# Unrolled layers, attention in pairs of heads, sigmoids on ScalarE and low weight parts on VectorE in a two-layer hybrid decoder

## Chip, cores and metric

One core of a Trainium2 chip runs the kernel. The metric is the device time of one launch in microseconds (us). Engines are called as in the profile: PE is TensorE, DVE is VectorE, ACT is ScalarE, POOL is GpSimd, SP is SyncE, which here only issues DMAs.

## What is computed

Two layers of a decoder trunk on 512 tokens of width 1024, in float32. A combined input projection feeds three kinds of token mixing (latent attention, called A; an mLSTM matrix memory, B; dilated sliding-window attention, C), then come cross-attention to 256 memory tokens and a SwiGLU of inner width 2816. Each sub-layer has an RMS norm before and one after it, ahead of the residual add.

```python
def reference(x, mem, w_in, ...):
    ...
    for l in range(DEPTH):
        h = rms_norm(x, norm_mix_pre[l])
        (c_q, c_kv, k_rope, ml_q, ml_k, ml_v, ml_o, ml_i, ml_f,
         sw_q, sw_k, sw_v) = jnp.split(h @ w_in[l], splits, axis=-1)
        y_a = mla_mixer(c_q, c_kv, k_rope, ...)          # 8 heads, dense causal, values of 64
        y_b = mlstm_mixer(ml_q, ml_k, ml_v, ml_o, ...)   # silu(conv(q, k)); sigmoid(ml_o) * h
        y_c = dilated_swa_mixer(sw_q, sw_k, sw_v, ...)   # 4 heads of 64
        y = jnp.concatenate([y_a, y_b, y_c], axis=-1) @ w_out[l]
        x = x + rms_norm(y, norm_mix_post[l])
        h = rms_norm(x, norm_x_pre[l])
        y = memory_cross_attention(h, rms_norm(mem, norm_mem[l]), x_w_q[l], x_w_kv[l], x_w_o[l])
        x = x + rms_norm(y, norm_x_post[l])
        h = rms_norm(x, norm_ffn_pre[l])
        y = swiglu(h, w_gate_up[l], w_down[l])
        x = x + rms_norm(y, norm_ffn_post[l])
    return x
```

## The kernel before

**Layout.** Activations are feature-major: `x` is 8 tiles (`KT`) of 128 features by 512 tokens, and all of them stay in SBUF. All 128 weight units of a layer (`N_UNITS`), each 128x1024 floats, stream through a ring of four slots (`RING`): units 0 to 21 are input, query, key and value weights of the mixing, from `U_OUT` = 22 the output projection, 30 and 38 the memory's keys and values, 46 the cross query, 54 the cross output, from `U_FF` = 62 gate and up, from `U_DOWN` = 106 the down projection.

**Three matmuls for one.** Every projection keeps nearly float32 accuracy with rounded operands: an operand is split into a high part and the rest, and PE adds three products (`three`, L552 hi by hi, L553 lo by hi, L554 hi by lo). So each unit takes three steps before PE can use it: SP loads it to `raw`, ACT makes `w_hi` (L853), and another engine subtracts to get `w_lo`. That is DVE (L1102) for units 2 to 21 and POOL (L522) for all from `U_OUT` on, and POOL (L451 and the layer's end) for units 0 and 1. A slot is loaded again once its low part is made; it is split again once PE has used the unit. Activations are split in the same way: ACT writes `h_hi`, DVE `h_lo` (L1152 for inputs whose norm factor is applied after the projection; L1128 and L1133, `tn_x` and `h_lo`, where it is applied ahead).

**Norms.** ACT squares a tile into one of two `sq` buffers (L865), DVE adds it to `acc` (L1112, L1114), PE sums over the partitions with a matrix of ones (L597), and ACT makes `rstd` with a logarithm and an exponential (L876). After an output projection, `residual` scales each `y` tile by `rstd` (L1163) and adds it to `x` (L1168); in the second and third residual, POOL adds tiles 1, 3, 4 and 6 (`POOL_ADDS`, L528).

**Order.** Each engine has its program written out by hand in blocks: a first block loads the memory and prepares the first units, then a hardware loop (`nc.Fori`) runs one block per layer and after it one that clears all semaphores of the layer, with a jump back; a last block stores `x` in one DMA (L1521). In a layer: `h_hi`/`h_lo` of all x tiles; the input projection, two output tiles together at first (L622 turns the first norm's factors right after the third tile); convolution and silu of the mLSTM's queries and keys; mLSTM loop of 16 steps (4 heads by 4 key blocks; spreads over four rows, scores L677, numerators L685, weights L1341) with the query, key and value projections between its steps; mixing attention of 12 heads (8 A, 4 C); output projection with the memory's norm; residual; keys and values of the memory, which PE can do without `x`; `x_pre` norm (first all eight squares, then eight norm steps); cross-query projection; cross-attention; its output projection; residual with the input of the FFN; FFN; down projection; residual.

**Sigmoids.** `silu` of the convolutions and the output gate are 1/(1+exp(-v)): ACT makes the exponential, DVE adds one and takes the reciprocal (`silu`, L1212 and L1326 for `o_gate`). In the FFN it is the same (L1477).

**Mixing attention** takes one head at a time, four query blocks each: PE scores (L747), DVE masks and takes the row's extreme (L1404), ACT exponentiates, DVE divides, PE transposes the probabilities (L725, three units behind), ACT copies them out, and two units later the head's value product (L753) runs over four key blocks, with an output of 64 partitions. DVE makes the head's `h_lo` (L1423).

## Time and profile before

| | |
|---|---|
| median of 3 runs | 1825.67 us (1823.3 to 1828.65) |
| profiled execution, its own time | 1825.33 us |
| its span in the trace | 1823.5 us |
| mean granted clock of PE | 0.954 |
| busy PE / DVE / ACT / POOL | 92% / 57% / 37% / 31% |
| moved by DMA | 146.5 MB, mean 80 GB/s |

One execution was recorded by the hardware profiler. Times in its rows are in us from the start of the span, if not marked ns. A group of instructions is named by its line in the kernel, its engine, and output<-inputs. In brackets behind a row stands how long the engine had waited before it and for which instruction. "Granted clock" is the share of full speed at which PE was let run: 1.00 is 2.4 GHz, 0.50 is 1.2 GHz. The rows themselves follow behind the change.

### The profile page before, as it was taken

Reading aid. Unit: us, or ns where it says so; the run is one execution under the profiler, and the core shown is the slowest. Engines: PE = TensorE matmul, PEld = TensorE weight load, DVE = VectorE, ACT = ScalarE, POOL = GpSimd, SP = SyncE. Lnnn points to the kernel's source line nnn. Section 1 sums busy time; section 2 is a strip of 40 time slices with the busy share of each in tenths; the row PEclk is TensorE's granted clock in tenths of the full one; section 3 lists DMA queues with packets and bytes.
Section 4 is the critical chain, followed back from the end, with each engine's and each line's share of the span. In section 5 each row is a group of like instructions: output and inputs, shape, how many; then the busy total and the mean of one; then the engine's idle time right before and its main releaser. Section 6 shows DMA issues by size and latency. Waiting matters only on the chain.

```text
span 1823.5 us, 20537 instructions
## 1 busy us (share of the span) xinstructions
PE 1669.0 (92%) x7040; PEld 1267.5 (70%) x7040; DVE 1046.6 (57%) x1511; ACT 675.2 (37%) x1148; POOL 565.9 (31%) x240
## 2 busy tenths in 40 slices
PE   6998899889989999999689988998899899999994
PEld 5864457767667888888468554477677678888883
DVE  5968872752257776600378678727531678765003
ACT  5322674444443332222143216644343432332221
POOL 1000103562234454444300001036613434444442
PEclk9989999999999999999889889998999999999997
DMA  5210002341112332223023110033412123222221
GB/s 224 93 60 33 24 1 104 105 137 59 58 46 91 105 102 95 102 93 103 25 95 104 36 35 13 1 116 105 137 47 69 55 84 109 98 96 100 102 95 58
DMA packets 39099, 146.50 MB, mean 80 GB/s; under 512 B 4976, under 2 KB 4976, under 8 KB 38256
## 3 DMA queue, kind: packets, MB, share of 16 engines
q1 hardware_dynamic: 39024, 145.53, 23.3%
q8 instruction: 44, 0.72, 0.2%
q14 instruction: 31, 0.25, 0.0%
HBM read 143.41 MB, written 2.10 MB: 80 GB/s over the span
## 4 chain that ended last, share of the span: by engine, by line
PE 41%; DVE 5%; issue 2%; POOL 1%; ACT 1%; DVEq 0%; POOLq 0%; ACTq 0%
PE bank L552 11%; PE bank L554 11%; PE bank L553 11%; PE bank L753 2%; PE bank L747 1%; POOL w_lo L522 1%; PE bank L725 1%; DVE tn_x L1128 1%; PE bank L794 1%; PE bank L784 1%; PE bank L677 1%; PE bank L685 1%; DVE y_f L1163 0%; DVE o_gate L1326 0%; PE bank L597 0%
## 5 line engine op out<-in xcount | busy, mean ns | idle before, releaser
L522 POOL TENSOR_TENSOR w_lo<-raw,w_hi 128x1024 fp32r<-128x1024 f32 x212 | 518.8, 2455 | 1175.9 <-ACT w_hi L853 1175.9
L552 PE MATMUL bank<-h_hi,w_hi 128*128 128x512 f32 x1312 | 534.4, 407 | 68.0 <-DVE h_lo L1152 39.9
L553 PE MATMUL bank<-h_lo,w_hi 128*128 128x512 f32 x1312 | 520.2, 396 | 0.0
L554 PE MATMUL bank<-h_hi,w_lo 128*128 128x512 f32 x1312 | 519.3, 396 | 0.0
L853 ACT ACTIVATE w_hi<-raw 128x1024 fp32r<-128x1024 f32 x256 | 268.1, 1050 | 223.9 <-PE bank L554 223.7
L552 PEld LDWEIGHTS bank<-h_hi,w_hi 128*128 128x128 f32 x1312 | 252.3, 192 | 140.5 <-issue 55.6
L553 PEld LDWEIGHTS bank<-h_lo,w_hi 128*128 128x128 f32 x1312 | 252.8, 193 | 55.6 <-issue 3.9
L554 PEld LDWEIGHTS bank<-h_hi,w_lo 128*128 128x128 f32 x1312 | 252.1, 192 | 53.8
L1114 DVE TENSOR_TENSOR acc<-acc,sq 128x512 f32<-128x512 f32 x86 | 73.3, 852 | 322.4 <-ACT sq L865 320.7
L1477 DVE RECIPROCAL acc<-acc 128x512 f32<-128x512 f32 x44 | 147.5, 3353 | 1.5
L552 PE MATMUL bank<-a_hi,w_hi 128*128 128x512 f32 x352 | 138.7, 394 | 0.0
L554 PE MATMUL bank<-a_hi,w_lo 128*128 128x512 f32 x352 | 138.0, 392 | 0.0
L553 PE MATMUL bank<-a_lo,w_hi 128*128 128x512 f32 x352 | 136.6, 388 | 0.0
L1079 ACT ACTIVATE a_hi<-sq 128x512 f32 (+1 forms) x44 | 27.8, 632 | 252.0 <-DVE sq L1481 252.0
L865 ACT ACTIVATE sq<-bank 128x512 f32<-128x512 f32 x48 | 28.7, 598 | 146.9 <-PE bank L554 146.9
L554 PEld LDWEIGHTS bank<-a_hi,w_lo 128*128 128x128 f32 x352 | 66.1, 188 | 15.5
L553 PEld LDWEIGHTS bank<-a_lo,w_hi 128*128 128x128 f32 x352 | 66.1, 188 | 14.8
L552 PEld LDWEIGHTS bank<-a_hi,w_hi 128*128 128x128 f32 x352 | 66.2, 188 | 13.1
L1404 DVE CUSTOM_DVE_ANT_0 p_x<-bank,consts 128x256 f32<-128x256 f32 x32 | 13.6, 425 | 90.3 <-PE bank L784 89.4
L1011 ACT ACTIVATE p_mix<-p_mix,stat 128x128 f32<-128x128 f32 (+1 forms) x96 | 53.6, 558 | 27.0 <-DVE stat L1404 26.7
L961 ACT ACTIVATE w_ml<-w_ml 128x512 f32<-128x512 f32 (+3 forms) x32 | 15.0, 470 | 130.4 <-DVE w_ml L1352 130.4
L1404 DVE CUSTOM_DVE_ANT_0 p_mix<-bank,consts 128x128 f32<-128x128 f32 (+1 forms) x96 | 47.2, 492 | 21.4 <-PE bank L747 15.5
(185 smaller groups left out, 2205.1 us busy)
## 6 DMA issues: line engine op xcount, KB each, us to landing
raw<-w_in SPq DMA_DIRECT2D x248, 512.0 KB, 3.3
raw<-first_in SPq DMA_DIRECT2D x12, 512.0 KB, 3.5
mem<-mem_in SPq DMA_DIRECT2D x3, 1024.0 KB, 4.9
x<-x_in SPq DMA_DIRECT2D x1, 2048.0 KB, 10.6
out<-x SPq DMA_DIRECT2D x1, 2048.0 KB, 6.3
consts<-c_in SPq DMA_DIRECT2D x1, 1728.0 KB, 14.3
gains<-g_in SPq DMA_DIRECT2D x2, 36.0 KB, 3.7
first_g<-first_g_in SPq DMA_DIRECT2D x3, 4.0 KB, 3.1
```

What stands on the lines that cost most here:

```text
L522: pool.tensor_tensor(w_lo[:, s, :], raw[:, s, :], w_hi[:, s, :].bitcast(F32), ALU.subtract).then_inc(split_lo, 1)
L552: pe.matmul(out_ap, l_hi, r_hi, start=start, stop=False)
L553: pe.matmul(out_ap, l_hi, r_lo, start=False, stop=False)
L554: return pe.matmul(out_ap, l_lo, r_hi, start=False, stop=stop)
L753: mm = pe.matmul(outs[head % 2][0:64, kb * P:SEQ], mix_head(head)["v"](kb), pt_mix[:, head % 2, kb, kb * P:SEQ], start=(kb == 0), stop=(kb ...
L853: act.activation(w_hi[:, s, :], raw[:, s, :], ACT.Copy)\
L865: act.activation(sq[:, c % 2, 0:width], src, ACT.Square).then_inc(squared, 1)
L1011: act.activation(probs[:, u % PROBS, 0:n], probs[:, u % PROBS, 0:n], ACT.Exp, scale=-1.0, bias=stat[:, 0, u:u + 1], accum_out=stat[:, 1, u ...
L1079: act.activation(a_hi[:, bass.ds(j * (2 * SEQ) + i * SEQ, SEQ)], f_a[:, i, :], ACT.Copy)\
L1114: ins = dve.tensor_tensor(acc[:, :], acc[:, :], sq[:, s, :], ALU.add)
L1404: done(dve.tensor_tensor_reduce(probs[:, u % PROBS, 0:n], score_ring[u % 4][:, 0:n], const(mask(u // TB) + SEQ - n, n), -scale(u // TB), 3 ...
L1477: step(dve.reciprocal(e, e), 2)
```

## The change

- **No loop over layers.** Both layers are written out in one block. Each semaphore counts on through the second layer (`count`, with the steps of a layer in `PER_LAYER`); no clearing, no first and last block. Inner loops of the FFN stay.
- **Start.** SP issues the first four weight units and the four quarters of `x` in turn; all gains come in one load. The memory for its norm factor is loaded behind unit 7 and its squares and column sums are made inside layer 0's input projection. Three output tiles are projected together (`HEAD`), with six banks in turn (`IN_BANKS`).
- **Layer handover.** The residual at the FFN's end also makes the next layer's `h_hi`, `h_lo` and squares (`next_input`). The result is stored in four quarters as its tiles are finished.
- **Latent norms.** The squares of the latent query and key tiles are summed over partitions by PE straight from `sq` (`latent_sum`), three matmuls for two, without an addition on DVE.
- **Sigmoids** outside the FFN: ACT makes exp, ln(1 + .), exp(-.) one after the other, and DVE only multiplies.
- **Low weight parts.** DVE makes units 4 to 65 (up to `U_FF` + 3), set beside its other work (`lo_until`, `beside`); POOL makes 0 to 3 and from 66 on. POOL adds nothing to `x` any more.
- **Mixing attention in pairs.** The steps of two heads go together (`pair_scores`, `pair_transposes`, `pair_out`); six probability buffers (`tn_mix` lends two). The value products of the two heads alternate and write partitions 0 to 63 and 64 to 127 of one bank, so one `h_hi`, one `h_lo` step serves a pair.
- **`x_pre` squares** are added inside the residual after the output projection (`x_square`).

```diff
-AHEAD = 2
-POOL_ADDS = (1, 3, 4, 6)
+HEAD = 3
+IN_BANKS = 6
 LAG = 3
 PROBS = LAG + 1
 OUT_LAG = 2
+PAIR_LAG = 2
+PAIR_PROBS = 2 * (PAIR_LAG + 1)
...
+    "mem_loaded": 16, "split_hi": N_UNITS, "split_lo": N_UNITS, "unit_used": N_UNITS,
+    "tile_done": tiles_done(len(USES) - 1),
...
+        def count(s, layer, n):
+            return layer * PER_LAYER[s.name] + n
...
+                for s in range(RING):
+                    sp.dma_start(raw[:, s, :], w_in[s, :, :]).then_inc(raw_loaded[s], 16)
+                    if s == 0:
+                        sp.dma_start(gains[:, :, :], g_in).then_inc(gains_loaded, 16)
+                    sp.dma_start(x[:, 2 * s:2 * s + 2, :], x_in[:, 2 * s:2 * s + 2, :]).then_inc(x_loaded[s], 16)
...
+                    for n in range(0 if layer else RING, N_UNITS):
+                        if layer == 0 and n == 2 * RING:
+                            sp.dma_start(mem_sq[:, :, :], mem_in).then_inc(mem_first, 16)
+                        if n == U_OUT + RING + 1:
+                            sp.wait_ge(mix_at["out_lo"], count(mix_at["out_lo"], layer, MIX_PAIRS))
+                            sp.dma_start(mem[:, :, :], mem_in).then_inc(mem_loaded, 16)
+                        load(first + n)
+                for i in range(KT // 2):
+                    sp.wait_ge(x_updated, count(x_updated, DEPTH - 1, N_SCALED - KT + 2 * i + 2))
+                    sp.dma_start(out[:, 2 * i:2 * i + 2, :], x[:, 2 * i:2 * i + 2, :]).then_inc(stored[i], 16)
...
+                def make_lo(u):
+                    pool.wait_ge(split_hi, u + 1)
+                    pool.tensor_tensor(w_lo[:, u % RING, :], raw[:, u % RING, :], w_hi[:, u % RING, :].bitcast(F32),
+                                       ALU.subtract).then_inc(split_lo, 1)
+                for layer in range(DEPTH):
...
+                    for n in list(range(RING)) + list(range(U_FF + RING, N_UNITS)):
+                        if n == U_FF + RING:
+                            pool.wait_ge(k_pe_ready, count(k_pe_ready, layer, 1))
+                            pool.wait_ge(ml_num, count(ml_num, layer, ML_HEADS * TB))
+                            pool.tensor_copy(k_mla[K_PE_ROWS[0], 2:MLA_HEADS, :], k_pe[K_PE_ROWS[0], :].unsqueeze(1)
+                                             .broadcast_to([MLA_ROPE, MLA_HEADS - 2, SEQ])).then_inc(k_pe_copied, 1)
+                            pool.wait_ge(k_pe_copied, count(k_pe_copied, layer, 1))
+                            wait_split(pool, layer, U_FF + RING - 1)
+                        make_lo(layer * N_UNITS + n)
...
-                    pool.wait_ge(k_pe_copied, 1)
-                    each_unit(pool, U_OUT + 2, U_FF + RING, make_lo)
-                    add_tiles("x_post", y_x)
-                    each_unit(pool, U_FF + RING, N_UNITS, make_lo)
...
+                    def latent_sum(name, first, n):
+                        pe.wait_ge(latent_squared, count(latent_squared, layer, first + n))
+                        pe.wait_ge(ln_done, count(ln_done, layer, NORM_AT[name]))
+                        for k in range(n):
+                            mm = pe.matmul(norm_bank[:, :], const(C_ONES), sq[:, k, :], start=(k == 0),
+                                           stop=(k == n - 1))
+                        mm.then_inc(norm_summed, 1)
...
                         after_norm("mix_pre")(k)
-                        for m in range(2):
+                        for m in range(HEAD):
                             project_step("in", m, k, tiles(h_hi), tiles(h_lo))
-                            if k == KT - 1 and m == 0:
-                                pe.wait_ge(consts_loaded, 16)
-                                norm_sum("mix_pre")
...
                         for kb in range(TB):
-                            mm = pe.matmul(outs[head % 2][0:64, kb * P:SEQ], mix_head(head)["v"](kb),
-                                           pt_mix[:, head % 2, kb, kb * P:SEQ], start=(kb == 0), stop=(kb == TB - 1))
+                            for i in range(2):
+                                mm = pe.matmul(outs[pair % 2][64 * i:64 * i + 64, kb * P:SEQ],
+                                               mix_head(2 * pair + i)["v"](kb), pt_mix[:, i, kb, kb * P:SEQ],
+                                               start=(kb == 0), stop=(kb == TB - 1))
                         mm.then_inc(mix_at["out"], 1)
-                    attention(mix_at, MIX_HEADS, p_mix, causal_len, mix_scores, mix_out)
...
-                    pe.wait_ge(mix_at["out_lo"], MIX_HEADS)
...
+                        if s < PAIR_STEPS:
+                            pair_scores(s)
+                        t = s - PAIR_LAG
+                        if t >= 1 and t % TB == 0:
+                            pair_out(t // TB - 1)
+                        if 0 <= t < PAIR_STEPS:
+                            pair_transposes(t)
...
-                        act.activation(o_gate[:, j, :], o_gate[:, j, :], ACT.Exp, scale=-1.0).then_inc(o_exp, 1)
+                        wait_emptied(act, layer, use_of("in", OG + j))
+                        e = o_gate[:, j, :]
+                        done(act.activation(e, e, ACT.Exp, scale=-1.0), act_step)
+                        done(act.activation(e, e, ACT.Ln, bias=one[:, :]), act_step)
+                        act.activation(e, e, ACT.Exp, scale=-1.0).then_inc(o_exp, 1)
...
+                def scaled_lo(layer, name, k, g):
+                    dve.wait_ge(normed_hi, count(normed_hi, layer, normed_before(name) + k + 1))
+                    done(dve.scalar_tensor_tensor(out=h_lo[:, k, :], in0=x[:, k, :],
+                                                  scalar=gains[:, layer, g + k:g + k + 1],
+                                                  in1=h_hi[:, k, :].bitcast(F32), op0=ALU.mult,
+                                                  op1=ALU.subtract), normed_lo)
...
-                        dve.wait_ge(conv_exp, j + 1)
-                        e = conv_in[:, j % 2, 3:3 + SEQ]
-                        done(dve.tensor_scalar(e, e, 1.0, None, ALU.add), dve_step)
-                        done(dve.reciprocal(e, e), dve_step)
-                        done(dve.tensor_tensor(ml_qk[:, j, :], ml_qk[:, j, :], e, ALU.mult), ml_qk_ready)
+                        dve.wait_ge(conv_exp, count(conv_exp, layer, j + 1))
+                        done(dve.tensor_tensor(ml_qk[:, j, :], ml_qk[:, j, :], conv_in[:, j % 2, 3:3 + SEQ], ALU.mult),
+                             ml_qk_ready)
...
-                    lo_until(U_OUT)
                     ml_denominator(ML_HEADS - 1)
                     ml_finish(ML_HEADS - 1)
                     for b in range(TB):
                         take_value(b)
                     ml_output_lo(1)
+                    lo_until(U_OUT + 3)
...
+                    dve.wait_ge(mem_loaded, count(mem_loaded, layer, 16))
                     mem_norm = (KT, tiles(mem), G_MEM, tiles(m_hi), tiles(m_lo))
-                    add_squares("mix_post", KT, between=lambda m: norm_step("mem", m, *mem_norm))
+                    add_squares("mix_post", KT, between=lambda m: norm_step("mem", m, *mem_norm),
+                                beside=lambda m: lo_until(U_OUT + m + 4))
...
+                    def x_square(k):
+                        lo_until(U_XK + k + 4)
+                        if k >= 1:
+                            add_square(layer, "x_pre", k - 1)
+                    residual("mix_post", "out", y_x, x_square)
+                    add_square(layer, "x_pre", KT - 1)
...
+                    dve.wait_ge(rstd_ready, count(rstd_ready, layer, NORM_AT["x_pre"] + 1))
+                    for k in range(KT + 1):
+                        norm_step("x_pre", k, KT, tiles(x), G_X_PRE, tiles(h_hi), tiles(h_lo))
+                        lo_until(U_XV + 7 + (k + 1) // 2)
...
+                    def next_input(k):
+                        if k >= 1 and layer + 1 < DEPTH:
+                            scaled_lo(layer + 1, "mix_pre", k - 1, G_MIX_PRE)
+                            add_square(layer + 1, "mix_pre", k - 1)
+                    residual("ffn_post", "down", y_f, next_input)
...
+                            dve.wait_ge(ff_lo, count(ff_lo, layer, j * 2 + (i + 1)))
+                    dve.wait_ge(rstd_ready, count(rstd_ready, layer, NORM_AT["ffn_pre"] + 1))
```

DVE, from the residual behind the output projection of the first layer to the first norm steps (y_x is the projection's output, acc and sq the sum and a tile of squares). Before:

```order
L1163 TENSOR_TENSOR y_x<-y_x,rstd 128x512
L1168 TENSOR_TENSOR x<-x,y_x 128x512
L1163 TENSOR_TENSOR y_x<-y_x,rstd 128x512
L1168 TENSOR_TENSOR x<-x,y_x 128x512 x2
L1112 COPY acc<-sq 128x512
L1114 TENSOR_TENSOR acc<-acc,sq 128x512 x7
L1128 SCALAR_TENSOR_TENSOR tn_x<-x,gains,rstd 128x512 x2
L1133 TENSOR_TENSOR h_lo<-tn_x,h_hi 128x512
L1128 SCALAR_TENSOR_TENSOR tn_x<-x,gains,rstd 128x512
L1133 TENSOR_TENSOR h_lo<-tn_x,h_hi 128x512
```

After, same place:

```order
L1250 TENSOR_TENSOR y_x<-y_x,rstd 128x512
L1254 TENSOR_TENSOR x<-x,y_x 128x512
L1231 TENSOR_TENSOR w_lo<-raw,w_hi 128x1024
L1173 COPY acc<-sq 128x512
L1250 TENSOR_TENSOR y_x<-y_x,rstd 128x512
L1254 TENSOR_TENSOR x<-x,y_x 128x512
L1231 TENSOR_TENSOR w_lo<-raw,w_hi 128x1024
L1175 TENSOR_TENSOR acc<-acc,sq 128x512
L1250 TENSOR_TENSOR y_x<-y_x,rstd 128x512
L1254 TENSOR_TENSOR x<-x,y_x 128x512
L1231 TENSOR_TENSOR w_lo<-raw,w_hi 128x1024
```

Each tile's scaling and add are now followed by a low weight part and the add of the last tile's square, where before no weight part stood on DVE and the eight squares came at the end.

PE, inside the mixing attention of group A in the first layer: scores from k_mla and q_mla, transposes of p_mix, value product from pt_mix and v_mla. Before:

```order
L747 MATMUL bank<-k_mla,q_mla 128x512
L725 MATMUL bank<-consts,p_mix 128x128
L747 MATMUL bank<-k_mla,q_mla 128x128
L725 MATMUL bank<-consts,p_mix 128x128 x2
L753 MATMUL bank<-pt_mix,v_mla 64x512
L753 MATMUL bank<-pt_mix,v_mla 64x384
L753 MATMUL bank<-pt_mix,v_mla 64x256
L753 MATMUL bank<-pt_mix,v_mla 64x128
L747 MATMUL bank<-k_mla,q_mla 128x256
L725 MATMUL bank<-consts,p_mix 128x128 x3
```

After:

```order
L732 MATMUL bank<-k_mla,q_mla 128x256 x2
L745 MATMUL bank<-consts,p_mix 128x128 x8
L732 MATMUL bank<-k_mla,q_mla 128x384 x2
L756 MATMUL bank<-pt_mix,v_mla 64x512 x2
L756 MATMUL bank<-pt_mix,v_mla 64x384 x2
L756 MATMUL bank<-pt_mix,v_mla 64x256 x2
L756 MATMUL bank<-pt_mix,v_mla 64x128 x2
L745 MATMUL bank<-consts,p_mix 128x128 x2
L732 MATMUL bank<-k_mla,q_mla 128x512 x2
```

Where a head's value product was four instructions with 64 output partitions between single scores and transposes, now eight stand together, two of each width, and scores and transposes come in twos as well.

DVE at the layers' border: the last tiles of the residual behind the down projection (y_f is its output). Before, where the block then ends:

```order
L1163 TENSOR_TENSOR y_f<-y_f,rstd 128x512
L1168 TENSOR_TENSOR x<-x,y_f 128x512
L489 UNCONDITIONAL_BRANCH
L1507 UNCONDITIONAL_BRANCH
L1510 ISA x20
L1496 UNCONDITIONAL_BRANCH
L488 REGISTER_ALU
L488 COMPARE_AND_BRANCH
```

After, the same residual of the first layer, near its start:

```order
L1250 TENSOR_TENSOR y_f<-y_f,rstd 128x512 x2
L1254 TENSOR_TENSOR x<-x,y_f 128x512
L1250 TENSOR_TENSOR y_f<-y_f,rstd 128x512
L1254 TENSOR_TENSOR x<-x,y_f 128x512
L1181 SCALAR_TENSOR_TENSOR h_lo<-x,gains,h_hi 128x512
L1173 COPY acc<-sq 128x512
L1250 TENSOR_TENSOR y_f<-y_f,rstd 128x512
L1254 TENSOR_TENSOR x<-x,y_f 128x512
L1181 SCALAR_TENSOR_TENSOR h_lo<-x,gains,h_hi 128x512
L1175 TENSOR_TENSOR acc<-acc,sq 128x512
L1250 TENSOR_TENSOR y_f<-y_f,rstd 128x512
```

The end of the block, 20 clearing instructions and the loop's branch stood between the last add and the next layer's first h_lo; now that h_lo and its square's add stand between the residual's own steps.

## Rows read from the trace of the kernel before

**Rows 1.** The page: busy time of each engine, share of the span, instructions.

```profile
PE 1669.0 (92%) x7040; PEld 1267.5 (70%) x7040; DVE 1046.6 (57%) x1511; ACT 675.2 (37%) x1148; POOL 565.9 (31%) x240
```

**Rows 2.** PE's waits: for whom: us, times, longest; then a window of the FFN.

```profile
PE bank L552 <- DVE h_lo L1152: 39.9, 4, 23.0
PE bank L552 <- POOL w_lo L522: 16.5, 5, 7.3
...
core 0: us, PE busy (x) PEld busy (x) DVE busy (x) ACT busy (x) POOL busy (x), PEclk, DMA share, GB/s
600.00:640.00 40.00, 40.00 (x178) 33.15 (x177) 31.55 (x29) 12.18 (x16) 18.98 (x9) 1.00 0.32 105
```

**Rows 3.** Start, order of time: start us, us, engine, line, what [idle before <-releaser].

```profile
7.79 6.02 PE L483 MATMUL bank<-mem_sq,ones_first 128*128 128x256 f32 x16 [7.79 <-ACT mem_sq L466]
8.66 4.65 POOL L451 TENSOR_TENSOR w_lo<-raw,w_hi 128x1024 fp32r<-128x1024 f32 x2 [8.21 <-ACT w_hi L469]
...
26.24 1.22 DVE L1102 TENSOR_TENSOR w_lo<-raw,w_hi 128x1024 fp32r<-128x1024 f32 x1
...
27.38 0.74 DVE L1152 SCALAR_TENSOR_TENSOR h_lo<-x,first_g,h_hi 128x512 fp32r<-128x512 f32 x1
...
39.77 1.05 PE L622 MATMUL bank<-consts,mix_rstd 1*128 1x1 f32 x8
```

**Rows 4.** Handover to the second layer, order of time, PE and DVE.

```profile
892.44 0.40 PE L554 MATMUL bank<-a_hi,w_lo 128*128 128x512 f32 x1
...
896.92 1.29 DVE L1163 TENSOR_TENSOR y_f<-y_f,rstd 128x512 f32<-128x512 f32 x2 [2.65 <-ACT rstd L876]
...
918.43 0.79 PE L552 MATMUL bank<-h_hi,w_hi 128*128 128x512 f32 x1 [22.98 <-DVE h_lo L1152]
...
940.35 1.05 PE L622 MATMUL bank<-consts,mix_rstd 1*128 1x1 f32 x8
```

**Rows 5.** Output to query projection, layer 0, order of time: POOL, then DVE.

```profile
333.30 16.71 POOL L522 TENSOR_TENSOR w_lo<-raw,w_hi 128x1024 fp32r<-128x1024 f32 x6 [6.49 <-ACT w_hi L853]
...
333.57 2.90 DVE L1168 TENSOR_TENSOR x<-x,y_x 128x512 f32<-128x512 f32 x1
...
374.47 4.59 DVE L1128 SCALAR_TENSOR_TENSOR tn_x<-x,gains,rstd 128x512 f32<-128x512 f32 x2 [8.44 <-ACT rstd L876]
...
394.16 1.42 DVE L1133 TENSOR_TENSOR h_lo<-tn_x,h_hi 128x512 fp32r<-128x512 f32 x2
```

**Rows 6.** mLSTM stage, order of time, then a window as in Rows 2.

```profile
120.71 3.35 DVE L1326 RECIPROCAL o_gate<-o_gate 128x512 f32<-128x512 f32 x1
...
152.36 0.79 PE L685 MATMUL bank<-w_ml,ml_v 128*128 128x128 f32 x2 [2.17 <-DVE w_ml L1341]
...
1087.56 2.49 DVE L1313 TENSOR_TENSOR o_gate<-o_gate,sq 64x512 f32<-64x512 f32 x1
...
1033.00:1037.00 4.00, 4.00 (x9) 2.11 (x9) 2.29 (x3) 1.58 (x2) 0.00 (x0) 0.50 0.01 2
```

**Rows 7.** Windows: four A heads, two C heads; DVE by shape; a product.

```profile
224.33:247.33 23.00, 23.00 (x104) 13.27 (x103) 19.55 (x69) 17.44 (x53) 0.00 (x0) 1.00 0.00 1
254.60:268.44 13.84, 13.84 (x53) 6.51 (x53) 9.74 (x35) 9.10 (x26) 0.00 (x0) 1.00 0.00 1
...
L1423 DVE TENSOR_TENSOR h_lo<-bank,h_hi 64x512 fp32r<-64x512 f32 x4 | 2.7, 683 | 0.1
...
L1404 DVE CUSTOM_DVE_ANT_0 p_mix<-bank,consts 128x256 f32<-128x256 f32 x4 | 1.7, 425 | 1.7 <-PE bank L747 1.7
...
247.67 2.37 PE L753 MATMUL bank<-pt_mix,v_mla 128*64 128x512 f32 x8
```

**Rows 8.** End, order of time; the page: DMA, count, KB, us to landing.

```profile
1812.54 0.69 DVE L1168 TENSOR_TENSOR x<-x,y_f 128x512 f32<-128x512 f32 x1
1816.44 0.35 SPq L1521 DMA_DIRECT2D out<-x  x1
...
raw<-w_in SPq DMA_DIRECT2D x248, 512.0 KB, 3.3
```

817 lines of the change are left out of this document (407 added, 410 removed).

## Prediction

> **What bounds the kernel now.** I read the page's first part, then who waits for whom on TensorE, then the order of time at the places where TensorE stands still. TensorE (PE) is busy 1669.0 of 1823.5 us [rows 1]; it sets the time, and the rest is gaps. The longest are on `h_lo` at the start and the layer handover (39.9 us in 4) and on low weight parts made by POOL (16.5 us in 5) [rows 2]. A second loss isn't idle time: in places PE runs at 1.2 GHz, granted clock 0.50 [rows 6], and does the same work in twice the time. In FFN and down projection it is dense at full clock, 178 matmuls touch a window of 40 us, 0.227 each [rows 2], and the change leaves them alone. The sum goes stage by stage, against the profiled execution's 1825.33 us, 0.34 below the median.
>
> **The change, part by part** (us; minus is gain; both layers together unless said).
>
> *Start: -6.9 +3.4.* Before, the third input tile is done at 39.7, where L622 follows [rows 3]. After, the memory's load and squares are out of the way, and three tiles are projected together. What is last is `w_hi[2]`: four activations on two x tiles stand ahead of each split on ACT (2.65), a split takes 1.0, so it is made by 4.2+1.0+2×(2.65+1.0)=12.5 (4.2: the first tile's landing, 3.3 after its issue [rows 8]), and POOL's low part takes 2.3 [rows 3]: 14.9. Then 66 matmuls, nine at half clock (3.9) and 57 at 0.228 (13.0), and the norm sum, 1.0: 32.8. The memory's column sums move from a time when PE had nothing to do into the dense stretch: 6.02 at half clock there [rows 3], 3.4 at full (8 matmuls, 256 columns, four passes). The latent norms' sums on PE add three fp32 matmuls for two, so 1 × 0.95 a layer: **+1.9**.
>
> *Handover: -17.9.* Last down matmul 892.44, `y_f` scaling from 896.92, first matmul of the next layer 918.43, its third tile done 940.4 [rows 4]. Block end, semaphore clearing and the jump back go; the next layer's `h_hi`/`h_lo` are made as each x tile is updated. DVE then does four steps a tile: scaling 0.65, add 0.69, `h_lo` 0.74 [rows 3, 4, 8] and the add of a square, as long as the other add; that is 2.77, and 2.82 from tile to tile with gaps; PE needs nine matmuls, 2.04: DVE paces. `h_lo[0]` at 901.0, `h_lo[7]` at 918.5, PE +2.0, norm sum +1.0: 921.5, against 940.4. POOL's last low part touches the first scalings: 1.0 back.
>
> *mLSTM stage: -15.* Six reciprocals a layer leave DVE, 3.35 each [rows 6]. The four of the convolutions buy nothing: PE is dense there and DVE only keeps up. The two output gates stand between mLSTM steps. Behind the second, PE stalls 2.17 in layer 0 [rows 6] and 2.24 at the same place of layer 1, and in stretches around such places it stays at half clock (0.50 in the window shown). In layer 0 the first gate is hidden by PE itself at half clock. From below: these stalls, 4.4. From above: the half-clock stretches also go, some 23 us in layer 0 and 34 in layer 1, half of each lost, 28 more. I take 12, near the low end, since the spread matmuls on four rows stay and half clock begins beside them too. With POOL quiet, DVE's slowed output product (2.49 for 0.69 [rows 6], and one like it in layer 0) gives 3. After the loop DVE makes three low parts (3×1.19) before the first mask, and loses 4.5 of slowing: nothing either way. ACT's new exp, ln, exp triples, two more steps of 0.65 each time, lie beside dense PE work on an engine that is 37% busy [rows 1]; without that cover they cost 1.3 each, 15.6.
>
> *Mixing attention: -18.* A head costs PE 5.75 (four in 23.0) in group A and 6.92 in C (two in 13.84), PE busy throughout [rows 7]. DVE is busy 19.55 in those 23.0 and waits 1.7 for scores, so unhindered it needs (23.0-1.7)/4=5.33 a head, less half an `h_lo` step (2.7/8=0.34): 4.99, 9.98 a pair. ACT is below that: 17.44/4=4.36. The value product, 2.37 for eight instructions on 128*64, i.e. half the array's columns [rows 7], becomes two interleaved ones on the two halves. No row shows whether they overlap: a pair costs 2.37 or 4.74. I take 2.37, since they share no column, output partition or operand. Then PE needs 11.5-2.37=9.1 a pair, DVE paces, and six pairs take 59.9 for 73.7 now: 13.8 a layer at best. I take 9: DVE, where it paces the mLSTM stage, is not gap-free, and a pair's drain adds a transpose group. If they don't overlap, group A gains nothing, C gains its halved switching between 64-row scores and full transposes (6.92-5.75=1.17 a head), the drain adds 2: about -2.5 a layer.
>
> The Trainium skill, "TensorEngine Tiling (Array Packing)", Key Properties, says that different tiles execute weight loads and matmuls in parallel; no run here shows it yet. By that the value product is the 2.37 I took.
>
> *Output projection to query projection: -26.* This is where POOL's low parts hurt twice. They come six in 16.71, 2.8 each, and DVE's adds beside them take 2.90 for 0.69 [rows 5, 8]. From 333.57 to 395.58 everything passes through DVE. After, DVE makes the parts itself, 1.22 each [rows 3]. Residual with squares: 0.61+0.70+1.19+0.72=3.2 a tile, 3.7 with the waits on ACT's squares (split 1.0, copy 0.4, square 0.6 are in line behind PE's 2.7 a unit); all squares added by 361, the fourth value unit's part 362, PE through it 364.8, sum 0.9, rstd 1.3: 367.0 where it was 374.47. Then eight steps of 1.51 and four parts of 1.19, `h_lo[7]` at 383.8: **11.8** less. Layer 1 took 4.8 longer for the same rows before, so 14.2 there.
>
> *FFN entry: -1.* DVE does all adds (2.82 a tile) but is no longer slowed. *End: -7.8.* Before: last add starts 1812.54, DMA issued 1816.44 after a block end [rows 8], span ends 1823.5. After: the last quarter is issued 0.4 after the last add's end (1812) and lands in 3.3 [rows 8]: 1815.7.
>
> **Sum:** -3.5+1.9-17.9-15-18-26-1-7.8=-87.3. **1738.**
>
> **Rivals.**
> 1. *Value products don't overlap.* For: PE's 64-row and full matmuls queue one by one in [rows 7]. Attention -5 for -18: **1751**. The Trainium skill, "TensorE: Matmul & The Clock Gate", The mechanism, says weight loads overlap running matmuls only when the row group differs; these halves share all rows. No row here shows it; by that the time would be this rival's.
> 2. *Full clock in the mLSTM stage.* With the gates gone PE has no gap over 1 us; -29 for -15: **1724**. Against: half clock also comes where PE was busy all the time, as in the window of [rows 6].
> 3. *DVE becomes the queue.* Low parts stand behind waits for squares: half of stage 5's gain and 7 of the mLSTM stage's are lost: **1758**.
> 4. *Slower.* A part waits for a split, that for PE's use of a unit, that for the part four ahead, with ACT's squares between. If ring slots didn't decouple them, each of 32 output and cross-output units (two layers) would take 1.22+1.05+5.44=7.7 for 5.44 and each of 32 key and value units 7.7 for 3.7: +72+128, **1938**; it passes 1825 from about 44% of that. Against: splits ran three units ahead in every stage.
> 5. *Nothing moves*, because the order compiled is the old one: 1825. The program's order speaks against it.
>
> **Chances.** Forecast 0.45 (its own range 1726 to 1746), rival 1 0.25, 2 0.12, 3 0.13, 4 0.03, 5 0.02. The range takes in 1 and 2 and, beyond 3, the lower ends of handover and attention (+10): **1716 to 1768**, leaving some 0.15 out. A measurement tells 0.3% apart; faster 0.95, same 0.02, slower 0.03.
>
> **What would show it.** Handover gap on PE near 8 us instead of 26. Value product of a pair near 2.4 and attention near 65 us a layer. No DVE step of 2.9 before the FFN. x_pre's first norm step 40 after the last output matmul, the last 57 after. Half-clock windows in the mLSTM stage fewer. Last `x` add to span's end 4 us. I am wrong if ACT's triples delay splits so that PE waits in the input projection, or if half clock spreads into attention once PE has slack there.

## The result and the profile after

The changed kernel takes **1755.38 us** (median of 4 runs, 1752.38 to 1756.94); the kernel before, run beside it, 1827.16 us. The ratio is 0.9608 with a 95% interval of 0.9591 to 0.9625. The profiled execution took 1754.44 us with a span of 1752.3, 71.2 less than the span before.

The page of the changed kernel, first the busy times, then two groups of its part on costly groups (busy us, mean ns):

```profile
PE 1631.1 (93%) x7044; PEld 1244.1 (71%) x7044; DVE 1027.5 (59%) x1568; ACT 677.8 (39%) x1156; POOL 325.5 (19%) x138
...
L489 POOL TENSOR_TENSOR w_lo<-raw,w_hi 128x1024 fp32r<-128x1024 f32 x132 | 319.8, 2427 | 1059.5 <-ACT w_hi L859 1059.5
...
L1231 DVE TENSOR_TENSOR w_lo<-raw,w_hi 128x1024 fp32r<-128x1024 f32 x124 | 150.9, 1225 | 101.9 <-ACT w_hi L859 90.0
```

PE is busy 37.9 us less than in [rows 1] and the gaps are 33.3 us less. POOL has 240 us less to do, and DVE makes 124 low parts at 1.22 us each.

Who waits for whom on PE (us in total, times, longest):

```profile
PE bank L510 <- DVE h_lo L1181: 21.1, 5, 8.9
PE bank L745 <- DVE p_mix L1510: 13.7, 14, 1.7
PE bank L510 <- DVE w_lo L1231: 7.5, 6, 1.3
PE bank L745 <- DVE tn_mix L1510: 6.1, 8, 0.9
```

The wait for `h_lo` is 21.1 us for 39.9 in [rows 2], and its longest is 8.9 for 23.0. The waits of transposes for probabilities of DVE, 13.7 and 6.1 us, are new: before, `p_mix` cost 3.8 us in all.

**Where the time went.** The order of time on PE and DVE has a row at each border. Those of the changed kernel, first layer and handover:

```profile
34.56 1.02 PE L557 MATMUL bank<-acc,consts 128*128 128x512 f32 x2
...
195.51 1.71 PE L732 MATMUL bank<-k_mla,q_mla 128*128 128x128 f32 x8
...
266.67 4.53 PE L756 MATMUL bank<-pt_mix,sw_v 128*64 128x512 f32 x16 [0.69 <-ACT pt_mix L1065]
...
359.52 1.54 DVE L1210 SCALAR_TENSOR_TENSOR tn_x<-x,gains,rstd 128x512 f32<-128x512 f32 x2 [2.42 <-ACT rstd L896]
...
425.12 3.60 PE L805 MATMUL bank<-pt_x,v_x 128*128 128x512 f32 x8
...
498.35 1.29 DVE L1250 TENSOR_TENSOR y_x<-y_x,rstd 128x512 f32<-128x512 f32 x2 [0.47 <-ACT rstd L896]
...
878.23 1.64 DVE L1250 TENSOR_TENSOR y_f<-y_f,rstd 128x512 f32<-128x512 f32 x2 [2.65 <-ACT rstd L896]
...
882.69 0.77 PE L510 MATMUL bank<-h_hi,w_hi 128*128 128x512 f32 x1 [5.94 <-issue]
...
903.05 1.02 PE L557 MATMUL bank<-acc,consts 128*128 128x512 f32 x2
```

The third input tile is done a norm sum after 34.56, at 35.6. That answers to the row at 39.77 in [rows 3], for L622 stands behind the third tile before and behind the fourth after.

| stage (from, to) | before, layer 0 / 1 | after, layer 0 / 1 | forecast, both | measured, both |
|---|---|---|---|---|
| start to third input tile | 39.8 | 35.6 | -6.9 | -4.2 |
| third tile to first attention score | 163.6 / 169.3 | 159.9 / 154.7 | -9.7 | -18.2 |
| attention, first score to last value product | 77.7 / 77.7 | 75.7 / 73.0 | -18 | -6.7 |
| to the first cross-attention value product | 164.9 / 163.5 | 153.9 / 153.9 | -26 | -20.6 |
| to the scaling of `y_f` | 450.8 / 450.7 | 453.1 / 452.9 | -1 | +4.4 |
| handover, `y_f` to third tile | 43.4 | 25.8 | -17.9 | -17.6 |
| last `y_f` scaling to the span's end | 22.0 | 13.7 | -7.8 | -8.3 |
| sum | | | -87.3 | -71.2 |

(The second row's forecast is mLSTM -15, latent norms +1.9 and the memory's column sums +3.4, which the prediction counted at the start.) Single stages in one profile differ by up to 3.5 us from kernel to kernel where nothing was changed in them: the second row's stage takes 154.7 us in layer 1 of the changed kernel and 154.8 to 158.2 in the eight kernels of experiments 1, 2, 7, 8, 9 and 10, which run the same program there. Its profile is the lowest of these, so some 2 us of that row's gain may be chance. The experiments are read with that in mind.

### The profile page after: what moved, and what is told of

It reads as the page before. It is cut to its first block, busy times and chain, and to the rows that moved or that the text cites. A ratio compares the mean times of both kernels' runs of the same rounds, so it can differ in the third digit from the quotient of the medians.

```text
span 1752.3 us, 19291 instructions
## 1 busy us (share of the span) xinstructions
PE 1631.1 (93%) x7044; PEld 1244.1 (71%) x7044; DVE 1027.5 (59%) x1568; ACT 677.8 (39%) x1156; POOL 325.5 (19%) x138
## 4 chain that ended last, share of the span: by engine, by line
PE 83%; DVE 10%; issue 3%; ACT 3%; DMA 0%; POOL 0%; SPq 0%; DVEq 0%; ACTq 0%
PE bank L510 24%; PE bank L512 23%; PE bank L511 23%; PE bank L756 2%; PE bank L805 2%; PE bank L732 1%; PE bank L795 1%; PE bank L658 1%; PE bank L666 1%; DVE p_mix L1510 1%; DVE x L1254 1%; DVE tn_x L1210 1%; PE bank L745 1%; PE bank L557 1%; DVE h_lo L1215 1%
## 5 line engine op out<-in xcount | busy, mean ns | idle before, releaser
L510 PE MATMUL bank<-h_hi,w_hi 128*128 128x512 f32 x1312 | 531.9, 405 | 47.9 <-DVE h_lo L1181 21.1
L489 POOL TENSOR_TENSOR w_lo<-raw,w_hi 128x1024 fp32r<-128x1024 f32 x132 | 319.8, 2427 | 1059.5 <-ACT w_hi L859 1059.5
L1175 DVE TENSOR_TENSOR acc<-acc,sq 128x512 f32<-128x512 f32 x84 | 64.2, 765 | 265.7 <-ACT sq L878 264.7
L1231 DVE TENSOR_TENSOR w_lo<-raw,w_hi 128x1024 fp32r<-128x1024 f32 x124 | 150.9, 1225 | 101.9 <-ACT w_hi L859 90.0
L498 POOL COPY k_mla<-k_pe 32x3072 f32<-32x3072 f32 x2 | 5.5, 2748 | 330.5 <-PE bank L666 330.5
L1581 DVE TENSOR_TENSOR sq<-bank,rstd 128x512 f32<-128x512 f32 x44 | 30.4, 692 | 49.8 <-PE bank L512 31.1
## 6 DMA issues: line engine op xcount, KB each, us to landing
consts<-c_in SPq DMA_DIRECT2D x1, 1728.0 KB, 13.7
```

The costliest lines, as they stand in the source:

```text
L489: pool.tensor_tensor(w_lo[:, u % RING, :], raw[:, u % RING, :], w_hi[:, u % RING, :].bitcast(F32), ALU.subtract).then_inc(split_lo, 1)
L510: pe.matmul(out_ap, l_hi, r_hi, start=start, stop=False)
L1175: ins = dve.tensor_tensor(acc[:, :], acc[:, :], sq[:, c % 2, :], ALU.add)
L1231: dve.tensor_tensor(w_lo[:, u % RING, :], raw[:, u % RING, :], w_hi[:, u % RING, :].bitcast(F32), ALU.subtract).then_inc(split_lo, 1)
L1581: dve.tensor_tensor(gate_up, ff_bank[2 * i][:, :], rstd[:, :], ALU.mult)\
```

## The experiments

Each is the changed kernel with one edit. Times are medians; ratios are to the kernel before, run beside it, with their 95% interval in brackets. The runs were made in several groups, so "slower" or "faster than the changed kernel" is the difference of the two ratios, in us.

**1. Scores ahead of the value product.**

```diff
-                        if s < PAIR_STEPS:
+                        t = s - PAIR_LAG
+                        value = t >= 1 and t % TB == 0
+                        if s < PAIR_STEPS and not (t >= 2 and t % TB == 1):
                             pair_scores(s)
-                        t = s - PAIR_LAG
-                        if t >= 1 and t % TB == 0:
+                        if value:
+                            if s + 1 < PAIR_STEPS:
+                                pair_scores(s + 1)
                             pair_out(t // TB - 1)
```

> Against the changed kernel, PE issues the scores of the next pair step ahead of a pair's value product instead of behind it. Coupling theory: in the changed kernel a pair takes 11.37 us though DVE is busy only 9.1 and PE 9.84 of them, because DVE stands 1.32 us waiting for scores that queue behind the 2.37 us value product, and PE later stands 0.66 and 0.70 us for the probabilities that come late through it. Then DVE's wait goes, a pair takes 10.0 to 10.3, and six pairs in two layers give 10 to 14 us: about 1743. Rival (PE itself or ACT is the limit, the waits are where slack shows): a pair stays at 11.2 to 11.4 and the time at 1753 to 1757.

Measured: 1759.72 us, ratio 0.9627 (0.9601 to 0.9653), about 3.5 slower than the changed kernel (the two intervals overlap, so what is shown is that nothing was gained). The theory fell as it was put. What it rested on is in the changed kernel's order of time, a pair in layer 1: PE, then one row each of DVE and ACT.

```profile
1085.96 2.37 PE L756 MATMUL bank<-pt_mix,v_mla 128*64 128x512 f32 x16
1088.26 0.44 PE L745 MATMUL bank<-consts,tn_mix 128*128 128x128 f32 x2
1088.54 1.88 PE L732 MATMUL bank<-k_mla,q_mla 128*128 128x512 f32 x4
1090.26 0.60 PE L745 MATMUL bank<-consts,p_mix 128*128 128x128 f32 x4
...
1091.96 1.20 PE L745 MATMUL bank<-consts,p_mix 128*128 128x128 f32 x6 [0.66 <-DVE p_mix L1510]
...
1094.73 1.38 PE L745 MATMUL bank<-consts,tn_mix 128*128 128x128 f32 x8 [0.70 <-DVE tn_mix L1510]
...
1089.69 0.69 DVE L1499 CUSTOM_DVE_ANT_0 tn_mix<-bank,consts 128x512 f32<-128x512 f32 x1 [1.32 <-PE bank L732]
...
1088.38 0.60 ACT L1054 ACTIVATE h_hi<-bank 128x512 fp32r<-128x512 f32 x1 [2.03 <-PE bank L756]
```

DVE waits 1.32 us for the scores at 1088.54, and PE 0.66 and 0.70 later. With the scores ahead, an A pair takes 12.03 us instead of 11.37 and a pair of group C 10.7 instead of 10.9 to 11.0. DVE and ACT show why nothing is gained:

```profile
1092.94 0.69 DVE L1502 CUSTOM_DVE_ANT_0 tn_mix<-bank,consts 128x512 f32<-128x512 f32 x1 [2.11 <-PE bank L745]
...
1092.55 0.60 ACT L1057 ACTIVATE h_hi<-bank 128x512 fp32r<-128x512 f32 x1 [3.75 <-PE bank L756]
```

The mask waits longer (2.11), now for transposes: it writes a probability buffer that only the transposes behind the value product free. ACT stands 3.75 us before `h_hi` of the pair, with this step's exponentials queued behind. So two further queues sat behind the value product.

**2. Value products head after head.**

```diff
-                        for kb in range(TB):
-                            for i in range(2):
+                        for i in range(2):
+                            for kb in range(TB):
```

> Against the changed kernel, a pair's eight value products are issued head after head, not alternating between the two halves of the bank; same instructions, same operands. If overlap of two products needs neighbours that write different halves of the output partitions, the 2.37 us group becomes about 4.4 to 4.7, a pair 13.4, and twelve pairs add 20 to 28 us: about 1780. If the 2.37 comes from something else (each product simply takes half the time when it is not between scores), the group stays at 2.4 and the time at 1755.

Measured: 1776.42 us, ratio 0.9728 (0.9698 to 0.9758), 22 us slower. The row of a pair on PE:

```profile
1097.18 3.93 PE L756 MATMUL bank<-pt_mix,v_mla 128*64 128x512 f32 x16
```

The same 16 instructions take 3.93 us for 2.37, and a pair 12.9 for 11.4. The overlap is real and needs neighbours that write different halves of the partitions. It is not twice 2.37, because a part overlaps even in this order. In the trace the second head's first instruction starts at 1098.74, 1.56 us behind the first head's first, and the last three of the first head start after it (1098.95, 1099.16 and 1099.27); 1.56 and 2.37 make the 3.93.

**3. The output gates' sigmoid back on DVE.** ACT makes one exponential, DVE adds one and takes the reciprocal at mLSTM steps 2 and 7.

```diff
+                        if u == 2:
+                            output_gate(0)
...
+                        if u == 7:
+                            output_gate(1)
```

> Against the changed kernel, the two output gates' sigmoid goes back to one exponential on ACT and add and reciprocal on DVE between the mLSTM steps, as before the change; everything else stays. Theory: the stage from the third input tile to the first attention score gained 22 us in two layers (without the memory's sums that moved into it) mainly because these 2 x 3.4 us a layer left DVE's chain there, directly and by less half clock; so 15 to 22 come back: 1770 to 1777, and PE stands about 2 us again behind the second gate. Rival: the gain is POOL's absence and the convolutions' reciprocals, then 0 to 6 come back: 1755 to 1761.

Measured: 1773.76 us, ratio 0.9703 (0.9677 to 0.9730), 17 us slower, as the theory had it. From third tile to first score it takes 166.8 and 165.3 us for 159.9 and 154.7. PE's longest wait for mLSTM weights is back (2.6 us, for 0.8 in the changed kernel), but the waits are the smaller part. PE is busy 157.7 and 157.2 us there for 153.7 and 148.5 with the same instructions, at a mean granted clock of 0.91 and 0.89 for 0.94 in both: 12.7 of the 17.5 us are PE's own time at the lower clock.

```profile
PE bank L666 <- DVE w_ml L1411: 6.4, 4, 2.6
```

**4. The convolutions' sigmoids back on DVE.**

```diff
-                        done(act.activation(e, e, ACT.Ln, bias=one[:, :]), act_step)
-                        act.activation(e, e, ACT.Exp, scale=-1.0).then_inc(conv_exp, 1)
...
+                        done(dve.tensor_scalar(e, e, 1.0, None, ALU.add), dve_step)
+                        done(dve.reciprocal(e, e), dve_step)
```

> Against the changed kernel, the sigmoids of the four convolutions go back to one exponential on ACT and add and reciprocal on DVE. By the prediction's step these buy nothing, since PE is dense there and DVE keeps up: 1754 to 1757. Rival: DVE, which also makes the low weight parts there, falls behind by some of its 16 us a layer, PE waits in the input projection or before the mLSTM's first scores, and 4 to 15 us come back.

Measured: 1771.83 us, ratio 0.9697 (0.9661 to 0.9733), 16 us slower. The rival was right, at a little more than it named:

```profile
PE bank L510 <- DVE o_gate L1239: 11.7, 2, 7.6
```

PE waits 4.1 us in layer 0 and 7.6 in layer 1 until DVE has emptied the gates' banks. DVE falls behind in the input projection and hands the delay to PE at its end.

**5. POOL makes the low parts of units 22 to 65.**

```diff
-                    for n in list(range(RING)) + list(range(U_FF + RING, N_UNITS)):
+                    for n in list(range(RING)) + list(range(U_OUT, N_UNITS)):
...
-                        while made_lo[0] < n:
+                        while made_lo[0] < min(n, U_OUT):
```

> Against the changed kernel, POOL makes the low weight parts of units 22 to 65 again (output projection to the FFN's first four units), DVE none of them; DVE keeps all adds. Theory: from the last value product to the cross-attention's first one the change gained 11.0 and 9.6 us, all of it from DVE making these parts itself in 1.2 us and not being slowed by POOL; so about 20 us come back here and 1 to 3 more in the mLSTM stage's end: 1775 to 1780, with DVE adds of 2.9 us beside POOL's parts. Rival: half of it is from the squares added inside the residual and from the unrolled order, which stay: 1763 to 1768.

The edit also puts POOL's copy of `k_mla` behind the parts of units 22 and 23, where it stood before the change.

Measured: 1788.84 us, ratio 0.9770 (0.9740 to 0.9801), 30 us slower, more than either theory. The four runs lie between 1782.9 and 1793.9, and the profiled one is among the long ones (1793.3), so the stages below add up to more than 30. PE's waits, and DVE beside POOL's parts (busy us, mean ns):

```profile
PE bank L512 <- POOL w_lo L489: 23.0, 8, 7.7
...
PE bank L512 <- DVE v_mla L1452: 8.1, 2, 4.1
...
L1256 DVE TENSOR_TENSOR x<-x,y_x 128x512 f32<-128x512 f32 x2 | 5.8, 2883 | 0.0
...
L1175 DVE COPY acc<-sq 128x512 f32<-128x512 f32 x1 | 2.5, 2514 | 0.0
```

From the last value product to the cross-attention's first it takes 165.1 and 166.7 us, 11.2 and 12.8 more than in the changed kernel. Another 8.2 and 9.0 us lie ahead of the attention. There DVE's copies of `k_mla` stand beside a low part of POOL, and its `ml_den` steps beside POOL's copy:

```profile
192.64 3.30 DVE L1380 TENSOR_TENSOR ml_den<-conv_in 64x256 f32<-64x256 f32 x2
...
200.13 0.80 PE L512 MATMUL bank<-w_hi,c_hi 128*128 128x512 f32 x1 [4.05 <-DVE v_mla L1452]
...
188.34 0.88 DVE L1378 TENSOR_TENSOR ml_den<-conv_in 64x256 f32<-64x256 f32 x2
```

Two steps of 64x256 take 3.30 us; in the changed kernel (last row), where POOL is idle then, 0.88. PE waits 4.05 us for what follows, 8.1 in the two layers. The other 9.0 of the 17.2 are PE's own longer busy time, at a mean granted clock of 0.91 in this stage for 0.94.

**6. POOL's low parts, and the squares behind the residual.** As 5, with

```diff
-                        if k >= 1:
-                            add_square(layer, "x_pre", k - 1)
...
+                    add_squares("x_pre", KT)
```

> As the kernel with POOL's low parts, and x_pre's eight squares are added after the residual instead of inside it, as before the change. DVE does the same work either way; inside the residual the adds fill time in which DVE would wait for nothing, so the order should matter only through the last square: the norm sum comes at most 5 us later a layer, 3 to 8 in all above that kernel. If POOL's parts set the pace in the residual, the adds inside it are hidden and the order matters fully: 10. If neither: 0.

Measured: 1785.35 us, ratio 0.9751 (0.9734 to 0.9769); by both time and span (1787.4 for 1791.2) nothing to 4 us faster than 5, and not the 3 to 8 slower that were expected. So the adds inside the residual are no gain of their own: beside POOL's parts they cost 2.5 us for 0.43 (the copy of the first square). Their worth with DVE's own parts wasn't tried, because there low parts and squares depend on each other through the two `sq` buffers.

**7. The FFN's inner activations at another address.** `a_hi` and `a_lo` lie 128, 384 or 512 bytes lower in each partition.

```diff
+        with ExitStack() as room:
+            room.enter_context(nc.sbuf_tensor("pad", [P, 128], F32))
+            a_hi = sb("a_hi", [P, FT * SEQ], F32R, room)
+            a_lo = sb("a_lo", [P, FT * SEQ], F32R, room)
         stat = sb("stat", [P, 3, MIX_UNITS])
```

> Against the changed kernel, only the two buffers of the FFN's inner activations lie 128 bytes lower in each partition, at the address they had before the change. In the down projection the matmuls follow one another in 0.2334 us in the changed kernel and in 0.2289 before, with the same instructions and clock. If the address of the moving operand sets this, the spacing returns to 0.2289, 1056 matmuls give 4.8 us: 1750.5. If the address of the weights (320 bytes higher than before, unchanged here), or the unrolled program sets it, 0.2334 stays and the time is 1755.

> Against the changed kernel, the FFN's inner activations lie 512 bytes lower in each partition; they are then 74880 bytes above the high weights, which leaves 128 when divided by 512, as in the changed kernel (75392) and unlike the run 128 bytes lower (75264, rest 0, spacing 0.2266 us) and the kernel before (75584, rest 320, spacing 0.2289). If the distance between weights and activations sets the spacing, it is 0.233 us again; if their own address does, anything else.

> Against the changed kernel, the FFN's inner activations lie 384 bytes lower; the distance to the high weights is 75008 bytes, rest 256 when divided by 512 and 0 when divided by 256. If the spacing depends on the distance modulo 256, it is 0.2266 us as at 128 lower; if modulo 512, it is another value, at 0.233 or above.

Windows of 40 us in the down projection, in the order before, changed kernel, 128 lower, 512 lower, 384 lower (the number in brackets behind PE's busy time counts matmuls that touch the window):

```profile
core 0: us, PE busy (x) PEld busy (x) DVE busy (x) ACT busy (x) POOL busy (x), PEclk, DMA share, GB/s
840.00:880.00 40.00, 40.00 (x176) 32.82 (x175) 2.94 (x3) 10.95 (x13) 18.45 (x8) 1.00 0.27 93
```

```profile
800.00:840.00 40.00, 40.00 (x173) 32.18 (x172) 1.39 (x2) 9.67 (x11) 16.80 (x7) 1.00 0.28 94
```

```profile
800.00:840.00 40.00, 40.00 (x178) 33.17 (x177) 2.10 (x3) 10.84 (x13) 17.80 (x8) 1.00 0.27 92
```

```profile
800.00:840.00 40.00, 40.00 (x173) 32.15 (x173) 2.05 (x3) 9.67 (x11) 16.90 (x8) 1.00 0.28 92
```

```profile
800.00:840.00 40.00, 40.00 (x178) 33.13 (x177) 2.11 (x3) 11.35 (x14) 16.78 (x7) 1.00 0.32 102
```

At full clock and with PE busy throughout, 176, 173, 178, 173 and 178 matmuls; from one start to the next 0.2289, 0.2333, 0.2266, 0.2333 and 0.2267 us. The distance from `w_hi` to `a_hi` by the order of the buffers is 75584, 75392, 75264, 74880 and 75008 bytes; divided by 256, it leaves 64, 128, 0, 128 and 0. The expected return to 0.2289 didn't come, the spacing fell below it. The kernel 128 lower takes 1747.23 us, ratio 0.9554 (0.9527 to 0.9582). 1056 matmuls by 0.0067 are 7.1 us. Measured were 10 by the ratios, 8 by the medians, 6.5 by the spans and 7.5 in the two stages that hold the down projection. The kernels 512 and 384 lower were timed once each, at 1757.85 and 1748.28 us, with spans of 1755.7 and 1746.2 for the 1752.3 and 1745.8 of the changed kernel and the one 128 lower. That it is the distance and not `a_hi`'s own address rests on the kernel before alone, where `a_hi` lies as in the kernel 128 lower and only the weights lie elsewhere.

**8. Mixing attention one head at a time**, with all other changes.

```diff
-                    for s in range(PAIR_STEPS + PAIR_LAG + 1):
+                    attention(mix_at, MIX_HEADS, p_mix, causal_len, mix_scores, mix_out)
```

> Against the changed kernel, the mixing attention is written one head at a time again, as before the change, with everything else changed. By the traces, from first score to last value product the stage took 77.7 and 77.8 us before and 75.7 and 73.0 after, so 6.8 in two layers should come back: 1762. If pairing also pushes work or half clock into the stages around it, the sum differs: a rival has pairs worth nothing (1755), because the low weight parts and copies ahead of the first pair, which take 15.8 us to the first value product for 9.4 before, would start earlier in single heads.

Measured: 1767.38 us, ratio 0.9669 (0.9642 to 0.9695), 11 us slower. An attention takes 81.1 us in both layers, so pairs gain 13.5 in the two, twice the 6.8 expected. For before the change single heads took 77.7. Two A heads, then one C head, in this kernel; then its wait at the start of an attention:

```profile
1088.97:1100.47 11.50, 11.50 (x53) 6.71 (x53) 9.78 (x35) 8.72 (x27) 0.00 (x0) 1.00 0.00 0
1126.16:1133.08 6.92, 6.92 (x27) 3.25 (x26) 4.88 (x18) 4.51 (x13) 0.00 (x0) 1.00 0.01 2
...
196.03 2.36 DVE L1171 TENSOR_TENSOR w_lo<-raw,w_hi 128x1024 fp32r<-128x1024 f32 x2
...
199.85 0.45 PE L706 MATMUL bank<-consts,p_mix 128*128 128x128 f32 x1 [3.23 <-DVE p_mix L1417]
```

PE waits 3.23 us for the first probabilities, for DVE makes two low parts (the row ahead of it) between the last `h_lo` of the mLSTM and the first mask. All of the 3.4 us lie there: from first score to first value product it takes 12.8 us for 9.4 before, and the rest of the attention is as long as it was. An A pair (11.37) is hardly shorter than two A heads (11.50); with C's heads it gains, 10.9 to 11.0 for two times 6.92.

**9. The next layer's input behind the residual.**

```diff
-                    residual("ffn_post", "down", y_f, next_input)
-                    next_input(KT)
+                    residual("ffn_post", "down", y_f)
+                    for k in range(1, KT + 1):
+                        next_input(k)
```

> Against the changed kernel, the next layer's low parts and squares stand on DVE behind the residual of the FFN, not between its steps; no block ends between the layers here either. DVE's sum of work is the same, but the first of PE's tiles can start only when all adds are done, and PE's 2.04 us a tile then follow DVE's 1.43: by the steps of the prediction 3 to 4 us come back: 1759. Rival: the fused order carries most of the 17.6 us that the handover gained, then 8 to 12 come back: 1763 to 1767.

Measured: 1762.18 us, ratio 0.9634 (0.9618 to 0.9650), 5 us slower; the handover takes 30.6 us for 25.8. By the step of the prediction (DVE's 2.8 a tile against PE's 2.04 behind it) 3 to 4 were expected, and the rival's 8 to 12 did not come.

**10. The value product's neighbours in another order, and the address of 7.** PE: scores, transposes, next scores, value product. ACT: exponentials ahead of `h_hi`.

```diff
                         if 0 <= t < PAIR_STEPS:
                             pair_transposes(t)
+                        if value:
+                            if s + 1 < PAIR_STEPS:
+                                pair_scores(s + 1)
+                            pair_out(t // TB - 1)
...
+                        if value and s < PAIR_STEPS:
+                            pair_exp(s)
+                        if value:
+                            pair_hi(t // TB - 1)
```

> The changed kernel with the FFN's inner activations 128 bytes lower, and with another order at a pair's value product: PE issues this step's scores, the transposes, the next step's scores and then the value product; ACT makes this step's exponentials ahead of the pair's high part. What the kernel with only the scores ahead showed: DVE's mask waits 2.11 us for transposes behind the value product, since it needs a free probability buffer, and ACT stands 3.75 us before the high part with exponentials queued behind it. Theory (head-of-line waits at the value product): both go, a pair falls from 11.37 to 10.0 to 10.4 us, 10 to 13 us in two layers, and with the lower address 1745.8 of that run's span becomes about 1734 (time 1736). Rival: the pair is bound by the round PE, DVE, ACT, DVE, PE of a step, whatever the order; pairs stay at 11.0 to 11.4 and the time at 1746.

Measured: **1740.08 us**, ratio 0.9527 (0.9500 to 0.9555), with span 1737.1, clear of the changed kernel's interval. Against the kernel with the lower address alone (0.9527 to 0.9582) it is not: 7 us by the medians, 9 by the spans, with overlapping intervals. What the order gives is read from the stage: the attention takes 70.0 and 69.9 us, for 75.5 and 75.8 there. An A pair, the interval in which C's scores begin, and PE's wait:

```profile
1079.00:1089.65 10.65, 9.35 (x53) 5.65 (x52) 9.09 (x34) 7.72 (x25) 0.00 (x0) 1.00 0.01 2
1099.64:1109.64 10.00, 8.36 (x55) 4.46 (x53) 9.10 (x34) 7.73 (x26) 0.00 (x0) 1.00 0.00 0
...
PE bank L746 <- ACT pt_mix L1069: 14.6, 20, 1.2
```

With C's scores an interval takes 10.00 (10.9 to 11.0 in the changed kernel), and no wait of DVE is listed in it: DVE's own pace, as the prediction had it (9.98). An A pair takes 10.65 (11.01 once), not the 10.0 to 10.4 expected, and DVE waits 0.8 us in it, for scores and for ACT. PE's waits are now for ACT's copies of the transposes, 14.6 us in 20: `pt_mix` has one buffer per head, so ACT can copy only behind the value product. A second one was not tried.

## Why the prediction was right, and where it wasn't

The time of 1755.4 lies in the range of 1716 to 1768, but 17 above the forecast of 1738 and outside the forecast's own 1726 to 1746. It is nearest to rival 3 (1758) and rival 1 (1751), and neither rival's mechanism is what happened. So the range held it in part by luck: it was wide enough for rivals that did not occur. By the table, 11.3 us are missing in the attention, 5.4 behind it, 5.4 in the stage of the down projection and 2.7 at the start, against 8.5 more than forecast in the mLSTM stage.

- **Handover and end** were right to 0.5 us: -17.6 and -8.3 for -17.9 and -7.8. Experiment 9 gives 5 us to the fused order, so some 13 of the 17.6 are left for what goes between the layers; that was not taken back by itself. PE's gap in front of the next layer's first matmul is 5.9 us for 23.0 [rows 4], and 8.5 us lie between it and the last down matmul, near the 8 that were to show it.
- **Start**: -4.2 for -6.9, a step mis-sized by 2.7 us. The third unit's low part let PE start at 16.5, not 14.9, after PE had waited 2.52 and 1.83 us for two of POOL's parts, and 15 matmuls instead of nine then ran at half clock. The memory's sums took 3.62 for 3.4. The latent sums on PE took 1.88 for 1.02, +0.9 a layer as forecast.
- **mLSTM stage**: without the sums -23.5 for -15. A part of this is where the border lies. The prediction set 4.5 us a layer of DVE's slowing beside POOL against three low parts, "nothing either way". Both sizes were about right, but they fall into different stages: the relief into this one, where PE's wait for `v_mla` went from 7.4 to 0.3 us, the low parts into the attention. That leaves 16.4 for 15, and here the number is right with a wrong make-up. The sign that "the four of the convolutions buy nothing" was wrong: experiment 4 gives 16 us for them alone, experiment 3 gives 17 for the gates alone, and experiment 5 shows 17 ahead of the attention for POOL's parts. They don't add up: together they gained 23.5, each alone taken back costs 16 to 17. What is put back on DVE, 7.6 and 14.8 us a layer by its busy time, passes into PE's time for a good part, as waits or as half clock. The failed step is that PE dense before the change was read as PE bound, with the reciprocals hidden; "DVE only keeps up" was the warning in the same sentence. In the changed kernel DVE is busy 32.2 and 33.9 of the first 40 us of the stage in the two layers and 32.2 of the last 40 in layer 0. The clock followed: the mean granted clock of the stage rose from 0.92 to 0.94 in layer 0 and from 0.89 to 0.94 in layer 1. The rows are PE's wait before and after, DVE's rows beside POOL before and the first of them after, then the last 100 us of layer 1 before and after (to the first scores).

```profile
PE bank L552 <- DVE v_mla L1386: 7.4, 2, 4.0
PE bank L510 <- DVE v_mla L1450: 0.3, 2, 0.2
...
189.69 3.46 DVE L1380 COPY k_mla<-k_pe 32x1024 f32<-32x1024 f32 x2
193.18 3.30 DVE L1304 TENSOR_TENSOR ml_den<-conv_in 64x256 f32<-64x256 f32 x2
...
186.90 1.41 DVE L1444 COPY k_mla<-k_pe 32x1024 f32<-32x1024 f32 x2
```

```profile
1012.00:1112.00 100.00, 86.07 (x235) 48.09 (x236) 77.34 (x104) 28.81 (x44) 10.25 (x4) 0.81 0.10 32
```

```profile
964.00:1064.00 100.00, 91.97 (x295) 54.30 (x294) 74.49 (x119) 31.66 (x51) 2.75 (x1) 0.91 0.11 37
```

- **Mixing attention**: -6.7 for -18. Of the 11.3 missing, 6.8 are the low parts ahead of the first mask, 3.4 us a layer (experiment 8: 81.1 for 77.7), which the prediction had counted with the stage ahead. Pairs by themselves gained 13.5, and the 4.5 missing there are the miss of the mechanism. That value products overlap (rival 1) was decided rightly: 16 instructions in 2.37 us, and by experiment 2 the order is the reason. The Trainium skill, "TensorEngine Tiling (Array Packing)", Key Properties, says that different tiles can execute weight loads and matmuls in parallel, and the traces agree, fully where the two halves alternate and for a part where they don't (3.93). What the prediction drew for rival 1 from the Trainium skill, "TensorE: Matmul & The Clock Gate", The mechanism, didn't come about: with all rows shared, 16 instructions took what 8 took before [rows 7]. The failed step is "PE needs 9.1 a pair, DVE paces": an A pair took 11.37 us with PE busy 9.84 and DVE 9.09, since each step passes PE, DVE, ACT, DVE and PE with few buffers, and a group of 2.37 us on PE holds back scores, transposes and, on ACT, exponentials. Experiment 10 took two of those queues away, brought the pairs with C's scores to the 9.98 of the prediction and the gain of pairs to 22.3 (70.0 and 69.9 for 81.1 twice). The last sign of being wrong, half clock spreading into the attention, came in a small way: in layer 0 the mean granted clock of the stage was 0.94 for 1.00 before, and its last value product took 4.53 us for the 2.37 of layer 1.
- **Output to query projection**: -20.6 for -26; by layer -11.0 and -9.6 for -11.8 and -14.2. Residual with parts and squares took 30.0 us from 322.4 to 352.4, as worked out (8 tiles at 3.7, 29.6). The last `h_lo` was done 53.7 us after the first scaling's start. The prediction's 383.8 is 51.4 after that of the kernel before (332.4), so this part came 2.3 later than put. In layer 1 the further 2.4 rested on a wrong reading: the DVE rows that take 62.0 us from 333.57 to 395.58 take 62.0 in layer 1 too. By experiment 5 POOL's parts are nearly all of it; the squares inside the residual are not.
- **FFN and down projection**: forecast as left alone, at 0.227 a matmul for both, which the row of [rows 2] shows for the FFN only. The change moves an address: `stat` lies between `w_hi` and `a_hi` and has 48 columns in place of 64, 192 bytes less. Each of 1056 matmuls takes 4.4 ns more, 4.6 us together. No row of the kernel before could show the loss, but the spacing there was 0.2289 for 0.2267 in the FFN: 1.2 us a layer that was there to be asked about.
